# Hybrid streaming encoder step: the 64 new sample frames' tile with two products instead of three, and work moved at the turn between the two passes

## The reference

```python
h = rmsnorm(x, norm_g);  proj = h @ w_in                  # 1024 -> 2832 columns
aq, ak, av, ag, gq, gk, gv, gg, glr, cv, cgl, cg = split(proj)
y_attn = band_attention(rmsnorm(aq), rmsnorm(ak), av, sinks) * silu(ag)   # band 128 + chunk of 64
o = gla_chunked(gq, gk, gv, logsigmoid(glr @ w_up + b) / 16, state)       # chunks of 64
y_gla  = rmsnorm(o, gla_g) * silu(gg)
u = cv * sigmoid(cgl);  c = causal_depthwise_conv(u, 31 taps) + conv_b    # 256 channels
y_conv = (silu(layernorm(c)) @ w_pw + b_pw) * silu(cg)
return x + concat(y_attn, y_gla, y_conv) @ w_out, new caches and states
```

## Time and profile before

| | us |
|---|---|
| three timed runs, median (lowest to highest) | 945.93 (945.79 to 946.61) |
| the profiled execution, its own time | 944.37 |
| span of its trace, first to last instruction | 942.6 |

### The profile page before, as it was taken

One profiled execution on the slowest core, in us unless ns is written; L12 is line 12 of the kernel. 1 busy time (PEld: TensorE's weight loads), 2 busy tenths in 40 slices (PEclk: granted clock), 3 DMA queues, 4 the chain that ended last, 5 costly groups with the idle time before them and its releaser, 6 DMA issues.

```text
span 942.6 us, 15963 instructions
## 1 busy us (share of the span) xinstructions
PE 901.9 (96%) x5713; PEld 807.9 (86%) x5713; DVE 787.3 (84%) x1906; ACT 475.2 (50%) x1168; POOL 204.1 (22%) x250
## 2 busy tenths in 40 slices
PE   6789999999999999999898999999999999999987
PEld 5667888888888888887897987999999899999965
DVE  6878888888888888889889989888788888878983
ACT  7666666677676666668573251241414223151401
POOL 0422222222221222220031330211203011120400
PEclk9899999999999999999999999999999999999999
DMA  9533222232333332135443221222120302112021
GB/s 314 191 120 112 97 105 96 96 113 102 111 112 112 112 112 90 68 118 140 108 123 101 69 68 57 57 70 66 40 95 1 118 18 79 57 46 91 1 79 59
DMA packets 57984, 87.79 MB, mean 93 GB/s; under 512 B 10065, under 2 KB 34513, under 8 KB 57905
## 3 DMA queue, kind: packets, MB, share of 16 engines
q1 hardware_dynamic: 57904, 86.77, 28.1%
HBM read 60.21 MB, written 26.60 MB: 92 GB/s over the span
## 4 chain that ended last, share of the span: by engine, by line
PE 79%; DVE 13%; ACT 4%; DMA 2%; issue 2%; SPq 0%; POOL 0%; POOLq 0%; DVEq 0%; ACTq 0%
PE J L691 23%; PE J L1928 18%; PE J L706 9%; PE J L2096 7%; DVE acc L1562 5%; PE J L2081 4%; PE S L1983 3%; PE T L2018 1%; PE T L2178 1%; PE S L2251 1%; PE J L2118 1%; DMA x_normed_scratch<-xraw 1%; PE S L2041 1%; DVE xbl L543 1%; PE S L2043 1%
## 5 line engine op out<-in xcount | busy, mean ns | idle before, releaser
L1562 DVE SCALAR_TENSOR_TENSOR acc<-ub,cwh,acc 128x256 f32<-128x256 f32 (+1 forms) x480 | 221.3, 524 | 0.2
L691 PE MATMUL J<-whi,xhi 128*128 128x512 f32 (+1 forms) x408 | 150.9, 370 | 8.7 <-DVE wlo L479 8.5
L1928 PE MATMUL J<-xbh,whi 128*128 128x256 f32 (+1 forms) x512 | 150.5, 294 | 2.7 <-DVE xbl L543 0.9
L691 PE MATMUL J<-whi,xlo 128*128 128x512 f32 (+1 forms) x408 | 146.8, 360 | 0.0
L691 PE MATMUL J<-wlo,xhi 128*128 128x512 f32 (+1 forms) x408 | 146.7, 360 | 0.0
L1928 PE MATMUL J<-xbh,wlo 128*128 128x256 f32 (+1 forms) x512 | 145.5, 284 | 0.0
L1928 PE MATMUL J<-xbl,whi 128*128 128x256 f32 (+1 forms) x512 | 144.6, 284 | 0.3 <-DVE xbl L543 0.3
L1928 PEld LDWEIGHTS J<-xbh,whi 128*128 128x128 f32 x512 | 96.4, 188 | 5.0 <-issue 2.3
L1928 PEld LDWEIGHTS J<-xbh,wlo 128*128 128x128 f32 x512 | 96.5, 189 | 0.4
L1928 PEld LDWEIGHTS J<-xbl,whi 128*128 128x128 f32 x512 | 96.1, 188 | 0.5 <-issue 0.5
L691 PEld LDWEIGHTS J<-whi,xhi 128*128 128x128 f32 x408 | 77.9, 191 | 20.3 <-DVE xlo L642 7.2
(11 more groups left out here) (273 smaller groups left out, 2255.8 us busy)
## 6 DMA issues: line engine op xcount, KB each, us to landing
out<-res SPq DMA_DIRECT2D x60, 256.0 KB, 2.0
x_normed_scratch<-xraw SPq DMA_DIRECT2D x17, 512.0 KB, 2.9
xtok<-in_x_prompt SPq DMA_DIRECT2D x16, 512.0 KB, 3.6
res<-in_x_prompt SPq DMA_DIRECT2D x16, 512.0 KB, 4.5
xbraw<-x_normed_scratch SPq DMA_DIRECT2D x16, 512.0 KB, 5.2
xraw<-xT SPq DMA_DIRECT2D x15, 512.0 KB, 3.5
res<-out SPq DMA_DIRECT2D x14, 512.0 KB, 4.4
wraw<-in_w_in SPq DMA_DIRECT2D x52, 128.0 KB, 2.4
```

Source lines behind the costliest of these rows:

```text
L691: last = nc.tensor.matmul(bank[:, 0:width], x[x_slot(ps, t)][:, k, :], w, start=(k == 0 and n == 0), stop=(k == KT - 1 and n == 2))
L1562: nc.vector.scalar_tensor_tensor(acc[:, j, 0:frames], src, w, acc[:, j, 0:frames], ALU.mult, ALU.add).then_inc(conv_step, 1)
L1928: last = nc.tensor.matmul(bank[:, 0:w], wt, x[:, k, 0:w], start=(k == 0 and m == 0), stop=(k == KT - 1 and m == 2))
```

## The change

**Sample tile.** `split_x_lo` and `y_lo_half` write the low part of tile 16 into the unused rows 64 to 127 of the high part's own tile, so that two products (against `whi` and `wlo`) give all terms, the upper 64 rows of the result being a separate addend. `evacuate` takes both halves with two instructions, and GpSimd adds them (`add_high`, twice for q/k/v and once for the gate). The attention of this tile does chunk 0 alone. The output product's upper half is taken by ScalarE (`take_rest`) and added by GpSimd (`add_rest`); likewise for the sample frames in block 1 (`take_rest_b`, `add_rest_b`).

**Second pass.** The low part of pair tile 1 of block 0 goes to GpSimd (`split_pair_lo_too`). Block 1's x has a buffer of its own, `xb1raw`, and is loaded and split earlier; VectorE makes both its low parts in front of `state(0, 0)`. `ln_scale` of all blocks but the last goes to ScalarE as `scale * x + bias`, for which GpSimd makes `-mean * factor` in two more small instructions; so do the first taps of block 0 (`first_tap`). In block 1 the projections begin in front of `gla_o(0, 1)`, and in block 2 `conv_T` stands behind `project_v(2, 0)`. The output products of blocks 0 and 6 (`output_gla_first`) begin with the GLA halves of both column halves, then `kend_T`, then the convolution halves.

```diff
-                for n, (x, w) in enumerate(((xhi, hi), (xhi, lo), (xlo, hi))):
+                products = ((xhi, hi), (xhi, lo), (xlo, hi))[0:2 if t.n == LAST else 3]
+                for n, (x, w) in enumerate(products):
...
+        def add_high(t, c, dst):
+            nc.gpsimd.wait_ge(A.taken[c], t.n + 1)
+            nc.gpsimd.tensor_tensor(dst[0:DEC, :], dst[0:DEC, :], low_part(c), ALU.add).then_inc(A.taken[c], 1)
...
+        def add_rest_b(h):
+            nc.gpsimd.wait_ge(o_low, 2 * TILES + 2 + h + 1)
+            nc.gpsimd.wait_ge(B.out_added, 2 * 2 + h + 1)
+            for n, part in enumerate((on[0:DEC, 2, :], gvt[0:DEC, 2, :])):
+                dst = res[0][0:DEC, h * 512 + n * 256:h * 512 + (n + 1) * 256]
+                last = nc.gpsimd.tensor_tensor(dst, dst, part, ALU.add)
+            last.then_inc(v_same, 1)
...
+            def ln_scale(g):
+                act.wait_ge(ln_r, gi + 1)
+                act.wait_ge(yg_lo, gi + 1)
+                for n, i in enumerate(own):
+                    last = nc.scalar.activation(cn[rows, i, :], bank[rows, 256 * n:256 * n + 256], ACT.Identity,
+                                                scale=rs[rows, i:i + 1], bias=nmr[rows, i:i + 1])
+                last.then_inc(cn_ready, 1)
...
+            def output_gla_first(p, b):
+                pe.wait_ge(yg_lo, groups_before(p + 1) if p > 0 else 1)
+                for h in range(2):
+                    output_half(empty_bank("out", p, h), 0, h, (0, 1), 0)
+                kend_T(b)
+                pe.wait_ge(yc_lo, groups_before(p + 1) if p > 0 else 1)
+                for h in range(2):
+                    output_half(bank_of("out", p, h), 0, h, (2, 3), 0).then_inc(slot_done, 1)
...
-                conv(0, 24, 30)
-                add_out(A, Tile(0, LAST), 0, bank_of("outa", LAST, 0))
-                state(0, 0)
-                split_pair_lo(1, 0)
+                conv(0, 24, 27)
+                split_pair_lo(1, 0)
+                split_pair_lo(1, 1)
+                state(0, 0)
+                conv(0, 27, 30)
+                add_out(A, Tile(0, LAST), 0, bank_of("outa", LAST, 0))
                 conv(0, 30, 32)
-                add_out(A, Tile(0, LAST), 1, bank_of("outa", LAST, 1))
                 state(0, 1)
                 mask_scores(0, 2)
-                split_pair_lo(1, 1)
+                add_out(A, Tile(0, LAST), 1, bank_of("outa", LAST, 1))
```

More of the change, by code:

```diff
@@ L317, in build @@
         rs = sb("rs", [P, 3])
+        nmr = sb("nmr", [P, 3])
         cn = on
@@ L488, in x_rows, with tokens, taken, chunks_of @@
             return src_p[0, bass.ds(t.n * P, P), cols], P
+        def tokens(t):
+            return DEC if t.n == LAST else P
+        def taken(t, c):
+            return A.taken[c], t.n + (2 if t.n == LAST else 1)
+        def chunks_of(t):
+            return (0,) if t.n == LAST else (0, 1)
+        def own_units(t, units):
+            return [u for u in units if u % 2 in chunks_of(t)]
+        def conv_steps(b):
+            return CJ * (CW * b - min(b, 1))
+        def y_low_at(at):
+            return WIDE + (at + DEC) % WIDE
         def x_slot(ps, t):
@@ L704, in output @@
                 hi, lo = weights(col, 512)
-                for n, (y, w) in enumerate(((yhi, hi), (yhi, lo), (ylo, hi))):
+                products = ((yhi, hi), (yhi, lo), (ylo, hi))[0:2 if t.n == LAST else 3]
+                for n, (y, w) in enumerate(products):
                     last = nc.tensor.matmul(bank[:, :], y[:, k, :], w, start=(k == 0 and n == 0),
-                                            stop=(k == 3 and n == 2))
+                                            stop=(k == 3 and n == len(products) - 1))
             last.then_inc(ps.out_psum, 1)
@@ L714, in add_out, with spare, add_rest @@
             nc.vector.wait_ge(ps.out_psum, 2 * t.n + h + 1)
[L715 to L716 removed]
+            rows = slice(0, tokens(t))
+            dst = res[t.par][rows, h * 512:(h + 1) * 512]
+            nc.vector.tensor_tensor(dst, bank[rows, :], dst, ALU.add).then_inc(ps.out_added, 1)
+        def spare(n):
+            return (cl, cth)[n][:, :, :].rearrange("p j n -> p (j n)")[0:DEC, 0:512]
+        def add_rest(h):
+            nc.gpsimd.wait_ge(o_low, 2 * TILES + h + 1)
+            nc.gpsimd.wait_ge(A.out_added, 2 * LAST + h + 1)
+            dst = res[Tile(0, LAST).par][0:DEC, h * 512:(h + 1) * 512]
+            nc.gpsimd.tensor_tensor(dst, dst, spare(h), ALU.add).then_inc(v_same, 1)
+        def add_rest_b(h):
[5 more added lines that the diff above has]
+            last.then_inc(v_same, 1)
         def go_count(g):
@@ L754, in empty_bank @@
             if n >= 3 and (kind, b, i) != ("out", NB - 1, 3):
-                nc.tensor.wait_ge(*emptied(*ORDER[n - 3]))
+                before = ORDER[n - 3]
+                nc.tensor.wait_ge(*emptied(*before))
+                if before[0:2] == ("outa", LAST):
+                    nc.tensor.wait_ge(o_low, 2 * TILES + before[2] + 1)
+                if before[0:2] == ("out", 0) and before[2] >= 4:
+                    nc.tensor.wait_ge(o_low, 2 * TILES + 2 + before[2] - 3)
             return bank_of(kind, b, i)
@@ L962, in _ @@
                         gate(b, n)
+                if b == 0:
+                    add_rest(0)
+                    add_rest(1)
+                if b == 1:
+                    add_rest_b(0)
+                    add_rest_b(1)
                 if b == NB - 1:
@@ L1150, in take_v, with first_tap @@
                 nc.scalar.activation(gvt[dst, i, :], bank_of("gv", b, i)[src, LR:LR + 256], ACT.Copy).then_inc(gv_taken, 1)
+            def first_tap(b):
+                frames = UB - HIST if b == 0 else 256
+                act.wait_ge(params_ready, 2 + CJ * b)
+                act.wait_ge(u_ready, 2 * b + 2)
+                act.wait_ge(hist_ready, b + 1)
+                need(act, cT_psum, groups_before(b))
+                for j in range(CJ):
+                    nc.scalar.activation(acc[:, j, 0:frames], ub[b % 2][:, j, 0:frames], ACT.Identity,
+                                         scale=cwh[:, j, 0:1], bias=convp[:, 0, j:j + 1]).then_inc(params_ready, 1)
             def take_gate(b, n):
@@ L1218, in conv_silu @@
                     cth_ready, 1)
+            def ln_scale(g):
+                gi, _, w, own = g
+                rows = slice(0, min(w, P))
+                bank = T[2] if own == (2,) else S[0]
+                act.wait_ge(ln_r, gi + 1)
[4 more added lines that the diff above has]
+                last.then_inc(cn_ready, 1)
             def y_hi(g, src, dst, scale, ready, done):
@@ L1379, in scores_max @@
                 def scores_max(n):
-                    for c in range(2):
+                    for c in chunks_of(t):
                         u = 2 * n + c
@@ L1548, in conv @@
                 frames = UB - HIST if b == 0 else 256
-                for n in range(a, e):
+                base = conv_steps(b)
+                by_act = CJ if b == 0 else 0
+                for n in range(max(a, by_act), e):
                     tap, j = n // CJ, n % CJ
@@ L2306, in _ @@
                 if b == 1:
+                    gla_o(0, 1)
+                    scores(0, 2)
+                project_b("cv", b, 0)
+                if b == 1:
+                    state_update(0, (2,))
+                project_b("cgl", b, 1)
+                if b == 1:
                     gla_o(0, 2)
-                project_b("cv", b, 0)
-                project_b("cgl", b, 1)
                 project_b("cv", b, 1)
```

340 lines of the change are left out of this document (222 added, 118 removed).

## The result

| | before | changed |
|---|---|---|
| timed runs, median (lowest to highest), us | 946.69 (944.39 to 950.01) | 942.24 (940.73 to 943.19) |
| ratio, 95% interval | | 0.9949 (0.9932 to 0.9966) |
| span of the profiled execution, us | 942.6 | 941.0 |

The change makes the kernel 0.5% faster, some 4.8 us by the ratio, where 13.3 were forecast. The time lies outside the range that was given. So the spans are not to be subtracted as they are.

What follows compares the result with a forecast made beforehand. TensorE was taken to bound the second pass's middle blocks, with TensorE and VectorE both near their limit in the turn. Terms -5.3, -4.1 and -3.9 sum to -13.3: 931.1 profiled, 932.6 us median; range 925.5 to 939.5.

Steps and rivals of the forecast that it cites:

- Term 1: Sample tile and block 0 up to the turned convolution: VectorE -6.8, additions +3, regained waits -1.5, together -5.3 us.
- The steps that named who decides: Up to block 0's turned convolution: whether TensorE's 8.4 us saving shows depends on VectorE, whose 62 taps the transpose needs.
- I take 3: Up to block 0's turned convolution: GpSimd additions lasting 10.5 us in all cost VectorE 3 us.
- The share of 0.4: From one earlier row, 0.92 us lost of 2.41: VectorE loses some 0.4 of the time beside a GpSimd addition.
- I take 1.5: Up to block 0's turned convolution: TensorE's idle time, which could shrink by 0 to 4.6 us, shrinks by 1.5.
- Term 2: Block 1: matmuls saved -1.85, TensorE's waits gone -2.8, additions +0.6, together -4.1 us.
- I allow 0.6: Block 1: the four GpSimd additions of the output sum hold the bank or VectorE, costing 0.6 us.
- Term 3: Last round: scaling off VectorE's chain and GLA halves filling TensorE's wait start the scores 3.9 us earlier.
- TensorE has no idle time there: 0: Blocks 2 to 6: moving the scaling, 0.99 us of VectorE a block, to ScalarE gains 0.
- The rival of the full stop: In the turn, GpSimd additions stop VectorE for their full length, giving 940.7 us; chance 0.20.
- The rival of the falling clock: In the turn, new waits of some 3 us lower TensorE's clock: 935.4 us, inside the likeliest case; no own chance.
- The starving of GpSimd: In the turn, VectorE delays awaited GpSimd links by 2.55 us each; eight late give 953 us; chance 0.04.

Runs made afterwards that it cites:

- blk1_old: Changed kernel with TensorE's old order in block 1 (first pointwise product between gk and gq, output product whole), last round kept new; ratio 0.9950 (0.9931 to 0.9969).

## Why the prediction was wrong

**Term 1 (-5.3 forecast, -2.9 measured, with a scatter of over 1 us).** The steps that named who decides were right, VectorE and not TensorE: 40 matmuls put back cost nothing. The step that failed is the price of the additions, "I take 3", and it failed in the reading of the earlier trace rows. There the VectorE instruction began at 413.21, when 1.33 us of the addition had passed, and ended at 414.56, 0.28 us (0.27 by the rounded row) behind the addition's end at 414.29. It could not lose 2.41 us, since only 1.08 were left; of these it lost 0.92. That is the mark of a full stop, and the prediction took it as evidence against one. The trace of the kernel before had it 15 times, once a tile, each time with the same 0.28 us; in every one the VectorE instruction began when the addition was under way. The share of 0.4 was thus of one overlap and not of an addition. Up to block 0's convolution the additions cost 2.3 us in three rows, 0.62 more in `osum` beside the low part (1.04 us for 0.42), and 2.0 in the taps, 4.9 together, instead of 3.

The second error is "I take 1.5" for regained idle time. TensorE did not begin block 0's projection sooner. It waited 2.05 us, and then ran at a clock of 0.79 from 440 to 448:

```profile
442.37 0.38 PE L2124 MATMUL J<-xbh,whi 128*128 128x320 f32 x1 [2.05 <-issue]
```

Before, that wait was 0.80, and the clock there 1.00. The projection begins 32.5 us behind the mark of tile 16, before it was 31.2. The link that grew is the one found above: GpSimd's low part holds `osum`, `osum` holds ScalarE's queue, and the last `xbh` stands in that queue. Without the low part on GpSimd the projection began at 30.7. Everything that term 1 gained, 4.3 us, it gained behind this point. The Trainium skill, GPSIMD Engine Reference, section 1 (Specifications), names contention with VectorE instructions in a 2-port perf mode or with two SBUF inputs; `osum<-osum,gth`, with two, agrees. `nmx`, 0.96 us for 0.17, has one, and whether it ran in such a mode no trace here shows.

**Term 2 (-4.1 forecast, +2.5 measured, +0.3 in two other profiles of the same instructions).** The matmuls and the state's wait went, but VectorE, not TensorE, ended the block. "I allow 0.6" for the additions was 1.9 of VectorE's time, in the taps that the next convolution waits for; I had priced them as a late bank. New waits of TensorE for `cl` (1.8), for the scaling on ScalarE (1.1, behind two more GpSimd links for the sample frames) and for taps (1.7) stood in no term. The change also moved both pointwise products behind `gq`, which the list under "The change" does not name. In three of five executions of the same block 1, the low clock added some 1.5 us.

**Term 3 (-3.9 forecast, -1.8 measured).** The chain was right, and the time that was missing is one wait and the low clock behind it: the second half's bank is that of `gk`. The text before says that each product waits for the bank of the third before it, and the term did not apply it. With `k_scaled` ahead, 57.0 us between the scores of the last blocks stand against 60.8 before, 3.8 less.

**The blocks and tiles (0 forecast, -1.7 and +1.2 measured).** The step "TensorE has no idle time there: 0" was right on idle time and on VectorE's 0.99 us. It left out that a tile of 12 bytes moves all buffers behind it.

The rival of the full stop came nearest, 940.7. It had the mechanism of the earlier trace rows right, if not the share of the additions under which VectorE had something to lose. That its sum came so near is in part luck: it had -0.8, -0.5 and -3.9 for the three terms, where -2.9, +2.5 and -1.8 were measured. Between 421 and 436 the additions' 0.79, 0.48 and 1.04 us of loss stand against durations of 1.27, 1.11 and 1.67. (Its term 2 takes 3.6 from -4.1, which holds 0.6 for the same additions already; without that it gives 940.2.) The rival of the falling clock came true as well, in both parts of the turn. The starving of GpSimd did not occur as written: two small links beside taps took 2.45 and 2.55 us, which took 1.96 and 1.76 before, and none of the ten additions more than 2.4.

What stays open: which operand's address makes the spacing of the matmuls, why the same wait is followed by a low clock in one execution and not in another, and what a kernel gains that keeps the two products and puts only GpSimd's low part elsewhere, which was not run.

## What to carry to other kernels

Where VectorE runs instructions in a row, an addition on GpSimd was paid by VectorE with about half of its length (0.43 to 0.62 of it here). So a product saved on TensorE is only a gain if its repair is on no busy engine: count the repair first. When a row shows one instruction beside another of a second engine, compare their ends, not only their lengths: an end that follows the other's end by the same time in every tile tells of a full stop. When an order is changed, walk the round of PSUM banks for every product that moves, and name the instruction that empties each. Compare stretches that the change doesn't touch, and when they differ, shift the buffers with nothing else changed. And before two traces are compared, look at the granted clock of the stretch and at a second profile of the same instructions: here that reversed what a pair of traces seemed to say of the order in block 1.

## What the runs showed of the hardware

A shift of all later SBUF buffers by 32 bytes changed the time of a steady block of some 400 matmuls from 54.53 to 54.80 us, and that of a tile of the first pass from 25.20 to 25.07, in opposite ways; another 32 bytes for the second pass alone gave 54.20, 0.6 us a block. Each number came out the same to 0.03 us in every kernel with the same layout. The same instructions of block 1 with the same 1.8 us wait were followed by a granted clock of 0.87 over 13 us (12 matmuls in 4.34 us) in three profiles and by 1.00 in two; the same wait of 2.52 us in the last round by 0.79 in the changed kernel and by 1.00 in blk1_old. A VectorE instruction with two SBUF operands that began beside a GpSimd instruction with two ended 0.28 us behind it, in 15 tiles of the kernel before and in nine profiles of the changed order, and took 1.03 to 2.12 us in place of 0.42. And a VectorE instruction of two columns with operands in SBUF took 0.96 us in place of 0.17 beside a GpSimd addition.
